# Forgetting-attention scores in fp32r: two heads on the row halves, high and low parts, three exponential buffers

## The reference, cut to what matters

```python
q = heads(q_in) * (dh ** -0.5)
k, v = heads(k_in), heads(v_in)
logf = jax.nn.log_sigmoid(f_pre.astype(f32)).transpose(0, 2, 1)
F = jnp.cumsum(logf, axis=-1)
...
    s = jnp.einsum('bhtd,bhsd->bhts', qb, k) + (fb[..., None] - F[:, :, None, :])
    s = jnp.where(pb[:, None] >= pos[None, :], s, -jnp.inf)
    p = jax.nn.softmax(s, axis=-1)
    return jnp.einsum('bhts,bhsd->bhtd', p, v)
```

## Time and profile before

| what | value |
| --- | --- |
| timed runs, median of 3 | 876.93 us (875.0 to 878.51) |
| profiled execution | 872.08 us, span 870.3 us |
| TensorE products busy | 847.0 us, 97% |
| VectorE busy | 438.8 us, 50% |
| ScalarE busy | 323.8 us, 37% |
| GpSimd busy | 48.2 us, 6% |
| granted TensorE clock over the span | 0.995 of full |

### The profile page before, as it was taken

How to read it: one execution, slowest core, us unless ns; L and a number is a source line. 1 busy time by engine, 2 the same in 40 slices (tenths; PEclk the granted TensorE clock), 3 DMA queues, 4 the chain that set the end, 5 groups by cost and what they waited for, 6 DMA issues and landing times.

```text
span 870.3 us, 10546 instructions
## 1 busy us (share of the span) xinstructions
PE 847.0 (97%) x3932; PEld 681.4 (78%) x3932; DVE 438.8 (50%) x703; ACT 323.8 (37%) x478; POOL 48.2 (6%) x75
## 2 busy tenths in 40 slices
PE   5999999999999999999999999999999999999996
PEld 3578888877787777787888778888888888888886
DVE  6789877247778654225873453333333333323222
ACT  4535445442323444343333553333333332222231
POOL 5310000000000000000001110000000000000110
PEclk9899999999999999999999999999999999999999
DMA  9833223348775121114234223333333333333322
GB/s 357 264 77 104 72 73 90 79 145 289 253 256 170 49 73 49 49 49 169 74 97 121 73 73 96 96 96 96 96 96 96 96 96 91 105 96 90 103 72 96
DMA packets 149372, 100.67 MB, mean 116 GB/s; under 512 B 11072, under 2 KB 142552, under 8 KB 148312
## 3 DMA queue, kind: packets, MB, share of 16 engines
q1 hardware_dynamic: 149128, 100.14, 37.9%
q10 hardware_dynamic: 208, 0.05, 0.0%
HBM read 97.03 MB, written 2.10 MB: 114 GB/s over the span
## 4 chain that ended last, share of the span: by engine, by line
PE 87%; DVE 5%; DMA 3%; ACT 2%; issue 1%; SPq 1%; DVEq 0%; ACTq 0%
PE bank L1696 25%; PE bank L1698 25%; PE bank L1697 25%; DMA raw<-in_w_in 3%; PE bank L1913 2%; PE bank L1843 1%; PE bank L1935 1%; PE bank L1863 1%; PE bank L1874 1%; DVE wlo L1190 1%; PE bank L1960 1%; ACT whi L696 1%; PE bank L1926 1%; PE bank L1911 1%; PE bank L1815 0%
## 5 line engine op out<-in xcount | busy, mean ns | idle before, releaser
L1696 PE MATMUL bank<-h_lo,whi 128*128 128x512 f32 x712 | 285.9, 402 | 1.8 <-DVE wlo L1190 1.0
L1698 PE MATMUL bank<-h_hi,wlo 128*128 128x512 f32 x712 | 278.1, 391 | 0.0
L1697 PE MATMUL bank<-h_hi,whi 128*128 128x512 f32 x712 | 277.9, 390 | 0.0
L1696 PEld LDWEIGHTS bank<-h_lo,whi 128*128 128x128 f32 x712 | 134.2, 189 | 32.2 <-issue 3.7
L1697 PEld LDWEIGHTS bank<-h_hi,whi 128*128 128x128 f32 x712 | 134.3, 189 | 28.7 <-issue 1.7
L1698 PEld LDWEIGHTS bank<-h_hi,wlo 128*128 128x128 f32 x712 | 134.1, 188 | 28.8
L1190 DVE TENSOR_TENSOR wlo<-raw,whi 128x1024 fp32r<-128x1024 f32 x60 | 73.3, 1223 | 104.7 <-ACT whi L696 104.7
L696 ACT ACTIVATE whi<-raw 128x1024 fp32r<-128x1024 f32 x60 | 63.2, 1055 | 151.3 <-PE bank L1698 107.8
L1698 PE MATMUL bank<-a_hi,wlo 128*128 128x512 f32 x176 | 68.5, 389 | 0.0
L1696 PE MATMUL bank<-a_lo,whi 128*128 128x512 f32 x176 | 68.5, 389 | 0.0
L1697 PE MATMUL bank<-a_hi,whi 128*128 128x512 f32 x176 | 68.5, 389 | 0.0
(11 more groups left out here) (334 smaller groups left out, 1005.8 us busy)
## 6 DMA issues: line engine op xcount, KB each, us to landing
raw<-in_ffn_w SPq DMA_DIRECT2D x60, 512.0 KB, 3.8
raw<-in_w_in SPq DMA_DIRECT2D x44, 512.0 KB, 4.0
slab<-in_mod_w SPq DMA_DIRECT2D x32, 512.0 KB, 5.9
modA<-in_mod_w SPq DMA_DIRECT2D x4, 1024.0 KB, 10.9
modB<-in_mod_w SPq DMA_DIRECT2D x4, 1024.0 KB, 18.4
raw<-in_w_out SPq DMA_DIRECT2D x8, 512.0 KB, 3.7
raw<-in_ffn_w SPq DMA_DIRECT2D x8, 384.0 KB, 3.2
xtok<-in_x SPq DMA_DIRECT2D x4, 512.0 KB, 5.6
```

What stands on the lines that cost most here:

```text
L1696: mm(dst, w_h, m_l, start=first, stop=False)
L1697: mm(dst, w_h, m_h, start=False, stop=False)
L1698: return mm(dst, w_l, m_h, start=False, stop=last)
```

## The change: what it does

The queries are kept as two heads in 128 rows, without zeros, and both queries and keys are split into high and low parts in fp32r: ScalarE makes `qhi` when it evacuates the chunk and `khi` in iterations 30 to 32, VectorE `qlo` in iterations 19 to 21 and `klo` in 30 to 32. A pair of heads is scored by eight fp32r products of 64 rows: the forget rows of each, then three part products of each, alternating between rows 0 to 63 (even head, bank 3) and rows 64 to 127 (odd head, bank 4). The forget rows and the selector are held a second time, at rows 64 and 96. The exponentials get a third buffer. Some buffers change places for this; the load of `w_glu` moves behind chunk 22's weights in SyncE's queue, since its new place is in use before. A zeroing of `qpad` on GpSimd goes away.

```diff
-        pf = at("pf", [P, 2, L], F32, X + 21.5)
+        pf = at("pf", [P, 3, L], F32, X)
-        wglu = at("wglu", [P, 2, S5W], F32, X + 4.5)
+        wglu = at("wglu", [P, 2, S5W], F32, X + 11.5)
-        qpad = at("qpad", [P, FH, L], F32, Z + 18.125)
+        qhi = at("qhi", [P, 3, L], F32R, Z + 18.125)
+        qf = at("qf", [P, 3, L], F32, Z + 24.125)
+        qlo = at("qlo", [P, 3, L], F32R, Z + 24.125)
+        khi = at("khi", [P, 3, L], F32R, 119)
+        klo = at("klo", [P, 3, L], F32R, Z + 30.125)
-        nft = at("nft", [42, 2, L], F32R, Z + 40.125)
+        nft = at("nft", [P, 2, L], F32R, Z + 40.125)
...
@@ SyncE
-            sp_.dma_start(wglu[:], w_glu.rearrange("(k p) n -> p k n", p=P)).then_inc(s_small, 16)
...
+                if s == 22:
+                    sp_.wait_ge(s_cx, 3)
+                    sp_.dma_start(wglu[:], w_glu.rearrange("(k p) n -> p k n", p=P)).then_inc(s_wglu, 16)
@@ GpSimd
-            nc.gpsimd.memset(qpad[:], 0.0).then_inc(s_pad, 1)
@@ ScalarE
                 elif kind == "fq":
-                    act.wait_ge(s_pad, 3)
-                    A(qpad[0:FD, 2 * i, :], src[0:FD, :], ACT.Identity, bias=bq8[0:FD, i:i + 1],
-                      scale=FD ** -0.5)
-                    A(qpad[FD:P, 2 * i + 1, :], src[FD:P, :], ACT.Identity,
-                      bias=bq8[FD:P, i:i + 1], scale=FD ** -0.5).then_inc(s_evac, 1)
+                    A(qf[:, i], src[:], ACT.Identity, bias=bq8[:, i:i + 1], scale=FD ** -0.5).then_inc(s_evac, 1)
+                    act.wait_ge(s_evac, s + 1)
+                    A(qhi[:, i], qf[:, i], ACT.Copy).then_inc(s_qhi, 1)
...
+            def fox_k_hi(i):
+                act.wait_ge(s_mqk, MH)
+                act.wait_ge(s_evac, A_CHUNKS.index(("fk", i)) + 1)
+                A(khi[:, i], kf[:, i], ACT.Copy).then_inc(s_khi, 1)
...
             def fox_exp(n):
-                if n >= 2:
-                    act.wait_ge(s_ft, n - 1)
+                if n >= 3:
+                    act.wait_ge(s_ft, n - 2)
...
-                A(pf[:, n % 2, 0:ln], ps[3 + n % 2][:, 0:ln], ACT.Exp, bias=nmx[:, n % 2:n % 2 + 1],
+                A(pf[:, n % 3, 0:ln], ps[3 + n % 2][:, 0:ln], ACT.Exp, bias=nmx[:, n % 2:n % 2 + 1],
...
+                if 30 <= t < 33:
+                    fox_k_hi(t - 30)
@@ VectorE
+                for r in (32, 64):
+                    link(V.tensor_copy(sel[r:r + 10, :], ident[r:r + 10, r:r + 10]))
+                V.tensor_copy(sel[96:106, :], ident[96:106, 96:106]).then_inc(s_rows_m, 1)
...
                 link(V.tensor_copy(n_hi, v))
-                V.tensor_tensor(nft[32:42, t % 2, 0:ln], v, n_hi.bitcast(F32), ALU.subtract).then_inc(s_nft, 1)
+                V.tensor_copy(row[64:74], v)
+                V.tensor_tensor(row[32:42], v, n_hi.bitcast(F32), ALU.subtract)
+                V.tensor_tensor(row[96:106], v, n_hi.bitcast(F32), ALU.subtract).then_inc(s_nft, 1)
+            def fox_q_lo(i):
+                dve.wait_ge(s_qhi, i + 1)
+                V.tensor_tensor(qlo[:, i], qf[:, i], qhi[:, i].bitcast(F32), ALU.subtract).then_inc(s_qlo, 1)
+            def fox_k_lo(i):
+                dve.wait_ge(s_khi, i + 1)
+                V.tensor_tensor(klo[:, i], kf[:, i], khi[:, i].bitcast(F32), ALU.subtract).then_inc(s_klo, 1)
...
+                if 19 <= t < 22:
+                    fox_q_lo(t - 19)
+                if 30 <= t < 33:
+                    fox_k_lo(t - 30)
                 if t in (32, 34, 36):
                     nft_row((t - 32) // 2)
@@ TensorE
-            def fox_scores(n):
+            def fox_score_pair(pair):
+                t, i = divmod(pair, FH // 2)
                 ln = P * (t + 1)
                 pe.wait_ge(s_nft, t + 1)
+                if pair:
+                    pe.wait_ge(s_fe, 2 * pair)
+                else:
+                    pe.wait_ge(s_mp, NT * MH)
+                    pe.wait_ge(s_qlo, 3)
+                if t == 0:
+                    pe.wait_ge(s_klo, i + 1)
+                tok = slice(t * P, (t + 1) * P)
+                heads = [(ps[3 + e][:, 0:ln], slice(FD * e, FD * e + FD)) for e in range(2)]
+                for e, (b, own) in enumerate(heads):
+                    h = 2 * i + e
+                    mm(b, sel[own, MH + h:MH + h + 1].broadcast_to([FD, P]), nft[own, t % 2, 0:ln],
+                       start=True, stop=False)
+                for q, k in ((qlo, khi), (qhi, khi)):
+                    for b, own in heads:
+                        mm(b, q[own, i, tok], k[own, i, 0:ln], start=False, stop=False)
+                for b, own in heads:
+                    mm(b, qhi[own, i, tok], klo[own, i, 0:ln], start=False, stop=True).then_inc(s_fs, 1)
...
-                    fox_scores(2 * p)
-                    fox_scores(2 * p + 1)
+                    fox_score_pair(p)
```

More of the change, by code:

```diff
@@ L173, in build @@
         cx = at("cx", [P, 3, L], F32, 119)
-        hm = at("hm", [P, 3, L], F32, 119)
+        khi = at("khi", [P, 3, L], F32R, 119)
         mqk = at("mqk", [P, 3, L], F32, 125)
@@ L195, in build @@
         msq = at("msq", [P, NT, MW], F32, Z)
+        hm = at("hm", [P, 3, L], F32, Z)
         mo = at("mo", [P, 3, L], F32, Z + 6.125)
         vf = at("vf", [P, NT, FW], F32, Z + 12.125)
-        qpad = at("qpad", [P, FH, L], F32, Z + 18.125)
+        qhi = at("qhi", [P, 3, L], F32R, Z + 18.125)
+        qf = at("qf", [P, 3, L], F32, Z + 24.125)
+        qlo = at("qlo", [P, 3, L], F32R, Z + 24.125)
         kf = at("kf", [P, 3, L], F32, Z + 30.125)
+        klo = at("klo", [P, 3, L], F32R, Z + 30.125)
         fz = at("fz", [36, L], F32, Z + 30.125)
@@ L220, in build @@
         assert Z + 46.125 <= 207.5
-        fox = at("fox", [P, 3, L], F32, X)
-        ym_lo = at("ym_lo", [P, 3, L], F32R, X + 6)
+        fox = at("fox", [P, 3, L], F32, X + 6)
+        ym_lo = at("ym_lo", [P, 3, L], F32R, Z)
         ys_hi = at("ys_hi", [P, 2, L], F32R, X + 13.5)
         ys_lo = at("ys_lo", [P, 2, L], F32R, X + 17.5)
-        yf_hi = at("yf_hi", [P, 3, L], F32R, Z)
-        yf_lo = at("yf_lo", [P, 3, L], F32R, Z + 6)
+        yf_hi = at("yf_hi", [P, 3, L], F32R, Z + 6)
+        yf_lo = at("yf_lo", [P, 3, L], F32R, X + 6)
         slab = at("slab", [P, 4, D], F32, 91)
@@ L292, in build @@
         s_evac = sem("w_in_chunk_out")
+        s_wglu = sem("w_glu_loaded")
+        s_qhi = sem("fox_q_hi")
+        s_qlo = sem("fox_q_lo")
+        s_khi = sem("fox_k_hi")
+        s_klo = sem("fox_k_lo")
         s_scal = sem("s5_scalar_inputs")
@@ L703, in evac @@
                 if kind == "f":
-                    act.wait_ge(s_small, 16 * 16)
+                    act.wait_ge(s_small, 16 * 15)
                     A(fz[:], src[0:36, :], ACT.Identity, bias=fbias[0:36, 0:1]).then_inc(s_evac, 1)
@@ L1377, in nft_row @@
                     dve.wait_ge(s_ms, NT * MH)
-                    link(V.tensor_scalar(nft[:], ones[0:42, 0:2].unsqueeze(2).broadcast_to([42, 2, L]), 0.0, None,
+                    link(V.tensor_scalar(nft[:], ones[:, 0:2].unsqueeze(2).broadcast_to([P, 2, L]), 0.0, None,
                                          ALU.mult))
@@ L1382, in nft_row @@
                 v, n_hi = tmpp[0:10, 0:ln], nft[0:10, t % 2, 0:ln]
+                row = nft[:, t % 2, 0:ln]
                 link(V.tensor_scalar(v, fcum[:, 0:ln], fcum[:, P * t:P * t + 1], -1.0, ALU.subtract, ALU.mult))
                 link(V.tensor_copy(n_hi, v))
-                V.tensor_tensor(nft[32:42, t % 2, 0:ln], v, n_hi.bitcast(F32), ALU.subtract).then_inc(s_nft, 1)
+                V.tensor_copy(row[64:74], v)
[7 more added lines that the diff above has]
+                V.tensor_tensor(klo[:, i], kf[:, i], khi[:, i].bitcast(F32), ALU.subtract).then_inc(s_klo, 1)
             def fox_max(n):
@@ L1829, in m_qk @@
                 pe.wait_ge(s_cx, 3)
-                pe.wait_ge(s_small, 16 * 16)
+                pe.wait_ge(s_small, 16 * 15)
                 if h:
@@ L1878, in glu @@
             def glu(n):
+                pe.wait_ge(s_wglu, 16)
                 pe.wait_ge(s_y5l, 16 * 16)
@@ L1898, in m_transposes @@
                 ins.then_inc(s_mt, 1)
-            def fox_scores(n):
-                t, h = divmod(n, FH)
+            def fox_score_pair(pair):
+                t, i = divmod(pair, FH // 2)
                 ln = P * (t + 1)
                 pe.wait_ge(s_nft, t + 1)
-                if n >= 2:
-                    pe.wait_ge(s_fe, n - 1)
+                if pair:
+                    pe.wait_ge(s_fe, 2 * pair)
                 else:
                     pe.wait_ge(s_mp, NT * MH)
-                    pe.wait_ge(s_evac, A_CHUNKS.index(("fk", 2)) + 1)
-                b = ps[3 + n % 2][:, 0:ln]
-                mm(b, sel[0:42, MH + h:MH + h + 1].broadcast_to([42, P]), nft[:, t % 2, 0:ln],
-                   start=True, stop=False)
-                mm(b, qpad[:, h, t * P:(t + 1) * P], kf[:, h // 2, 0:ln], start=False,
-                   stop=True).then_inc(s_fs, 1)
+                    pe.wait_ge(s_qlo, 3)
```

(3 more changed lines are left out.)

3 lines of the change are left out of this document (1 added, 2 removed).

## The result

The changed kernel took 867.7 us (median of five executions, 867.2 to 869.93), against 876.0 for the kernel before (median of four, 874.55 to 878.51; the 876.93 of the table above is the median of three of them). The ratio of the two kernels is 0.9918, with a 95% interval of 0.9889 to 0.9947. That is 0.8% faster, beyond the 0.5% that this measurement can tell from no change. Forecast were 868.5 us, in a range of 864.5 to 874.5. One execution of the kernel before (953.35 us) and one of E1 (943.25 us, clock 0.845) were in a slower state and are left out of all medians and ratios.

The account below looks back on a forecast made before the run. TensorE, busy 97% of the span, was taken as the bound. Score blocks -10.8, waits +1.7, +0.8, +0.2 and -0.3 made -8.4 us: 863.7 profiled, plus 4.85 to the median, 868.5 us; range 864.5 to 874.5.

Parts of the forecast that it names:

- Side by side, but with stationary loads one after another: TensorE's score blocks, the case chosen: halves overlap, loads take turns; blocks total 14.0 us, saving 10.8; chance 0.36.
- loads side by side too: TensorE's score blocks, the low end: products and loads of both halves overlap; blocks total 10.2 us, saving 14.6.
- first pair (key part 2 in iteration 32): Before the first score pair: VectorE waits for ScalarE's key copy, delaying the last mLSTM weighting; new wait 1.7 us.
- chain to the transposes at t = 2: Longer forget rows add 0.76 us, nearly cancelled by ScalarE's work coming 0.6 earlier; wait up by 0.2 us.
- chunk 37 to 38 (forget rows of t = 3): One more cast and subtraction on VectorE, 0.95 us against slack of 0.15, delay TensorE's transpose; new wait 0.8 us.
- outputs at 335: At 335.05 TensorE's 0.29 us idle goes because ScalarE's copy comes earlier; -0.3 us.
- rival 4: Score stage bound by VectorE and ScalarE: full overlap partly given back at waits, 866.2, or doubled waits, 870.9; chance 0.16.
- The term of -0.6 on its chain: Third exponential buffer: ScalarE's exponential at 288.35 stops waiting for transposes; the next weights' high part comes 0.6 us earlier.
- The distance of 4.85 us: Gap between the kernel before's profiled execution (872.08) and timed median (876.93), kept to turn 863.7 into 868.5 us.
- Rival 1: Score blocks: a half can't load its next stationary while multiplying; blocks total 16.0 us, saved 8.8, time 870.5; chance 0.18.
- Rival 2: Score blocks: the halves don't run side by side; saved 6.0 less 2.4 of waits, time 873.3; chance 0.2.
- rival 3: Score blocks: each alternation empties the array, 0.2 us for each of seven changes; time 886.7, slower; chance 0.1.

Follow-up runs that it names:

- E1: Changed kernel with the third key part made one iteration earlier (parts 1 and 2 in iteration 31): 862.97 us, ratio 0.9863 to the kernel before.
- E8: The changed kernel run again, with nothing altered, as a measure of what repeats: 865.84 us, ratio 0.9909 to the kernel before.
- E7: Kernel before with only the third exponential buffer and the moved buffers and w_glu load: 873.48 us, ratio 0.9987 to the kernel before.
- E3: Changed kernel with the exponentials in two buffers again instead of three: 879.59 us, ratio 1.0051 to the kernel before.
- E10: E1 with products ordered head by head and TensorE waiting between heads for the even head's last product: 873.89 us, ratio 0.9998 to the kernel before.
- E2: Changed kernel with all four products of the even head issued first, then the odd head's four: 867.33 us, ratio 0.9922 to the kernel before.
- E6: E1 with VectorE's later forget rows (t = 2, 3) and mLSTM outputs moved behind the row maxima: 859.76 us, ratio 0.9828 to the kernel before.
- E9: E5 with VectorE's iterations 36 and 39 reordered as in E6: 859.62 us, ratio 0.9827 to the kernel before.
- E11: The kernel of E6 run again beside others on the same chip: 859.01 us, ratio 0.9827 to the kernel before.
- E5: Changed kernel with one float32 product of 64 rows per head and no high and low parts: 864.34 us, ratio 0.9890 to the kernel before.

## Why the prediction came out right

**The score block: direction and main mechanism right; size 2.9 us short.** "Side by side, but with stationary loads one after another" held in its first half and failed in its second. The loads go side by side as well, so the blocks took 11.1 us and not 14.0; saved 13.7 instead of 10.8. That is the second of the four cases, "loads side by side too", which had 0.52, 0.74, 0.96 and 1.18 (10.2 us in all): it is within 0.05 us from t = 1 on and 0.18 low at t = 0, where a step of two records takes 0.11 us (295.29, 295.40, 295.51) and not the 0.055 of the columns alone. The mis-sized term is the load-bound step at t = 0 to 2: 0.70, 0.77 and 1.01 for 1.15; at t = 3 it was exact, 1.22. The remark that "at N = 128 a block hardly changes" (1.15 for 1.27) is wrong with it: it fell from 1.27 to 0.70.

**The new waits: 4.0 us instead of 2.4 (4.3 in E8's profile).**

| place | forecast | measured |
| --- | --- | --- |
| first pair (key part 2 in iteration 32) | +1.7 | +2.1 |
| chain to the transposes at t = 2 | +0.2 | +1.1 (2.1 for 0.30 and 1.01) |
| chunk 37 to 38 (forget rows of t = 3) | +0.8 | +0.9 |
| outputs at 335 | -0.3 | -0.1 (0.20 for 0.29) |

TensorE's idle time in the stage grew by less than the 5 us that would have spoken against the forecast. The third wait is at another place: `fo` waits behind the forget rows on VectorE, and TensorE meets it at the values (L1979) and not at the transposes. The second is the step of the waits that failed. VectorE's rows of the changed kernel for t = 2:

```profile
301.25 0.35 DVE L1404 CAST nft<-tmpp 10x384 fp32r<-10x384 f32 x1
301.62 0.55 DVE L1405 TENSOR_TENSOR nft<-tmpp,nft 10x384 fp32r<-10x384 f32 x1
302.18 0.55 DVE L1406 TENSOR_TENSOR nft<-tmpp,nft 10x384 fp32r<-10x384 f32 x1
```

The added cast and subtraction take 0.94 us start to start (0.38 and 0.56), where 0.76 stood (at t = 3 it is 1.13 for 0.95). On ScalarE the third buffer gave 0.47 against the start of the score block, not 0.6 (0.73 in E8's profile, where the wait shown here is absent):

```profile
295.18 1.06 ACT L706 ACTIVATE whi<-raw 128x1024 fp32r<-128x1024 f32 x1 [0.66 <-PE bank L1733]
```

The exponential no longer waits, but the weights' high part behind it then waits for TensorE's chunk. And the block ahead of the wait is 0.55 us shorter, which is given back there: 0.94 - 0.47 + 0.55 is 1.0, beside 1.1 measured. The giving back is what rival 4 described; it was left out of the forecast's own sum. In E8's profile the block before the other wait (chunk 33) is given back too: that wait is 0.88 us for 0.30.

**The third buffer.** The term of -0.6 on its chain came out as -0.47 in the changed kernel, and as -0.55 alone (E7, 0.46 for 1.01). "Shortens nothing else" is right against the kernel before (E7) and misses its part in the change: a pair that waits at its head for two exponentials needs it (E3, 12 us).

**The rest.** The query parts, the moved `w_glu` load and the wider selector cost nothing that a wait or E7 shows. The sum by blocks and waits is -9.7 for a forecast -8.4; the two errors, 2.9 and 1.6 us, have opposite signs. The distance of 4.85 us from the profiled execution to the median was the clock: the two groups of executions of the kernel before, at 0.994 to 0.995 and at 0.988 to 0.991, lie 4.3 us apart. It didn't carry over (the changed kernel's median is 2.2 below its profiled time, and that profiled time is 869.93 where the forecast had 863.7), because the clock of the profiled executions was 0.995 in one and 0.987 in the other. So the direction and most of the size were right for the stated reason, while the hit to 0.8 us was luck in part: two errors that nearly cancel, and an offset that stood for a difference of clock, which the forecast did not separate.

**The rivals.** Rival 1 (a half can't load while it multiplies) falls by the loads at 355.58 and by blocks below its 1.15 to 1.62. The Trainium skill, TensorE: Matmul & The Clock Gate, The mechanism, has in its list a load overlap a running product only in another row group, though the same section also lets a load into the background weight buffer go ahead; the trace disagrees with the first, with loads 0.01 us behind the start of a product in their own half and the next product after 0.23 us. Rival 2 (not side by side) and rival 3 (each alternation empties the array) fall by the pairs; E10 made rival 2 come true by force, and the time was then that of the kernel before, where 873.3 was forecast for it. Rival 4 came nearest in mechanism, though its own name is wrong: neither VectorE nor ScalarE became the bound, but the loads overlap fully and gain is given back at both of the waits that it named (both seen in E8, one in the first profile). Its -10.7 us and the forecast's -8.4 lie on either side of the -9.7 by blocks and waits (-9.4 with E8's waits).

**Left open.** How often, and by how much on average, the wait before the first pair lowers the clock: E8 had 0.93 in the first window and E2 1.00, both with the 2.1 us wait. In E10 the clock fell once more at the second block of t = 3 (0.92 in the window from 349 to 393), and so it did in E1 and E2 (0.96 in the same window), each time with no wait of TensorE near it, but behind 16 products of a single column (`late_mod`, 1.84 us) and some of 64 and 128 columns; the changed kernel's own profile has the same products there and 1.00. Kernels with more idle time in the stage tend to lower clocks (0.984 to 0.988 in E3, 0.990 to 0.995 in E6, E9 and E11), but the kernel before, with little idle time, was seen at 0.988 to 0.991 as often as at 0.995, and no experiment changed the clock alone with a separated time.

## What to carry to other kernels

Two products of 64 rows on different row halves, into different banks, cost TensorE the time of one, alternating or head by head, as long as no wait stands between them; where an operand is half zeros, take the zeros out first, and split into fp32r parts only if the float32 form on the halves is shown to be slower. A tighter block is worth what the engines around it let through: look at what stands ahead of the row maxima on VectorE, since moving four small things behind them brought some 3 us, and one key part made earlier some 2 us before that. Compare executions, profiled or timed, only with their granted clocks beside them: 0.995 and 0.99 are 4.3 us apart for the same kernel.

## What the runs showed of the hardware that was not expected

- The two row halves run their records independently of the program's order between them (E2: 1.24 us a block head by head, 1.22 alternating). The Trainium skill, TensorEngine Tiling (Array Packing), Key Properties, says that tiles load and multiply in parallel; the trace agrees.
- Float32 products overlap on the halves just as fp32r ones do: 0.94 us for two of 64x512 (E5).
- A load starts in a half 0.01 us after a product started in it (355.58 and 355.57), and the product that needs it starts after the usual 0.23 us.
- The block with 64 rows costs about 0.1 us at its start and 0.2 us at its end beyond its columns: 0.33 us from the first pair to the second (355.24 to 355.57), 0.31 from the last pair to L1731 and 0.34 from there to L1732, where 0.23 is usual. The first record on either side starts together with its own load. That the change of row count is the cause is the likely reading, not a tested one.
- An idle stretch of 2.1 us on TensorE was followed by the 1.2 GHz level in three profiles (0.50 from 272 to 276 in the first, and again in E8 and E3) and by none of it in a fourth (E2, 1.00).
